# Turning normalised rows in 32x32 blocks on VectorE and in the loads, instead of on TensorE, for two of four token groups

## The chip, the cores and the metric

One core of a Trainium2 chip runs the whole program. The metric is the device time of one launch in microseconds; the median of three runs before the change was 2038.86 us (2037.51 to 2039.26).

## The reference, cut to what matters

One decoder layer over 2048 prompt positions and 64 sample positions, width 1024, in fp32. The part that matters here is the hand-over from the mixer to the MLP:

```python
x = layer_norm(DEEPNORM_ALPHA * x + g1 * mix, ln1_g, ln1_b)
h2 = x * (1.0 + sc2) + sh2
f = jnp.einsum("btf,fd->btd", jnp.square(jax.nn.relu(jnp.einsum("btd,df->btf", h2, w_up))), w_down)
x = layer_norm(DEEPNORM_ALPHA * x + g2 * f, ln2_g, ln2_b)
```

The mixer's output rows have tokens on partitions, since the norm runs along the features. The up projection needs h2 with features on partitions. Something has to turn the rows.

## The kernel before, in words

**Two phases.** The 2048 prompt positions are four groups (`SUPERS` = 4) of 512 (`GT`), four tiles of 128 rows each; the 64 sample rows are a fifth tile of the last group. First all four groups go through the mixer (`mixer(s)`, L1367 on PE and L1900 on VectorE), then all four through the MLP. Between the phases the normalised rows rest in DRAM, in `x_norm`, one row per position.

**Weights.** Every weight passes as a slab of 512 KB (128 partitions x 4 KB), in one fixed order numbered g. SP loads slab g into one of three raw buffers (L645), once POOL is done with slab g - 3. ACT copies it to the high part (`hi_part`, L1007), once PE is done with slab g - 4, of four slots. POOL subtracts to get the low part, in two halves (`lo_part`, L903). PE multiplies high by high, high by low and low by high (`mm3`, L1241 to L1243). A mixer has 24 slabs: 0 to 3 for v, 4 to 15 feature slabs (F0 to F11), 16 to 23 the output projection. A product slab of the MLP ("K", 12 matmuls of 512 columns) is one of seven products of a Strassen step on the down projection; an up slab ("U") has 24 matmuls. A group's MLP has 8 blocks of 4 U and 7 K. `mlp_order` (L65) fixes the order: U0 U1 K0 K1 U2 K2 K3 K4 U3 K5 K6 inside a group, with the K of the block before; at the end of a group seven K slabs stand in a row and then four U.

**The end of a mixer.** VectorE forms the residual and the statistics of each tile (L1893, L1895, L1658). ACT normalises tiles 0 and 1 in `xt` (`o_normal`, L1079), VectorE tiles 2 and 3 (L1668). The affine of this norm is folded into `scale2` and `bias2` for the MLP's input and applied on its own for the residual. In the next mixer SP stores the four tiles to `x_norm` behind slab 9 (`store_n`, L704) and reloads `xt` with the next residual behind slab 13. SP's queue also carries, into the third mixer, jobs that prepare sums of the down weights (L660, L674). VectorE writes the mixer's results to `mix` (`mix_out`, L1780) from feature slab F2 on; when it waits, its later evacuations of PSUM wait with it, and PE waits for those in turn by a ring of four banks.

**The start of an MLP group.** Group 0 is turned on PE while the last mixer ends. For groups 1 to 3, `next_n` (L801) loads the four row tiles of the coming group into four tiles that are free then (`next_rows`, L414: `gs`, `xt` tile 4, and two thirds of `rows`): tiles 0 and 1 behind U3 of the sixth block, 2 and 3 behind U3 of the eighth. After the last two K slabs of the seventh block and the first six of the eighth (`feature_after`, L121), PE turns one feature tile of 128 x 512 with four transposes of 128 x 128 into PSUM bank 2 or 3 (`n_transposes`, L1553; L1561), ACT applies `scale2` and `bias2` in place (`n_features`, L1137; L1141) and copies the high part to `hA` (L1145), VectorE subtracts for the low part (`n_feature`, L1707; L1711). The up projection of the next group waits for each of the eight parts (L1479).

**Order.** Nothing is scheduled by a planner: each engine's order is written out by hand, and SP is one queue in which an instruction that waits holds up every later transfer, the weight slabs among them.

Of the kernel before, what the change touches and what calls it, by code (L numbers as in the profile page):

```python
# [5 lines left out]
F32 = mybir.dt.float32  # L6
# [144 lines left out]
O_PAIRS = [(2, 3), (0, 1), (6, 7), (4, 5)]  # L151
MIX_ORDER = [0, 2, 3, 6, 1, 7, 4, 5]
# [148 lines left out]
def decoder_layer_kernel(nc, x_prompt, x_sample, x_turned, xs_turned, c_turned, conv_turned, pool_turned,  # L301
# [3 lines left out]
                         mod_rows, x_norm, w_mix):  # L305
    ctx = ExitStack()
    with ctx:
# [55 lines left out]

        ada_early = nc.alloc_sbuf_tensor_at("ada_early", [P, 2, KD, ADA_COLS], F32, offset=mix0)
# [124 lines left out]
        n_stage = sem("n_stage")  # L489
        n_in = [sem(f"n_in{t}") for t in range(5)]  # L490
# [90 lines left out]
        def _(sp):  # L581
# [123 lines left out]

            def store_y(s, t):
# [66 lines left out]
            for s in range(1, SUPERS):  # L773
                for n in range(MIX_SLABS):
                    slab(MIX_SLABS * s + n)
                    if n == 9:
                        store_n(s - 1)
                    if n == 13:
                        sp.wait_ge(n_stored, 64 * s)
                        load_residual(s)  # L780
# [20 lines left out]
            def next_n(s, t):  # L801
# [3 lines left out]
                elif s:  # L805
                    sp.wait_ge(n_tr, KD * s)
# [4 lines left out]
                sp.dma_start(next_rows[t], n_rows(s + 1, t)).then_inc(n_stage, 16)  # L811

            def load_n(s, t):
# [3 lines left out]
                if t == 4:  # L817
                    sp.wait_ge(n_tr, KD * (SUPERS - 1))
# [6 lines left out]
            for n, (kind, b, i) in enumerate(MLP_ORDER):  # L825
# [16 lines left out]
                else:  # L842
                    if (r, i) == (1, 1):

                        sp.wait_ge(n_tr, KD * s)
# [149 lines left out]
        def _(act):  # L995
# [141 lines left out]
            def n_features(e, k):  # L1137

                act.wait_ge(n_tr, KD * (e - SUPERS - 1) + k + 1)
                x = ps[:, 2 + k % 2, :]  # L1140
                act.activation(x, x, ACT.Identity, bias=bias2[:, k, 0:1], scale=scale2[:, k, 0:1]  # L1141
# [20 lines left out]
            for s in range(SUPERS):  # L1162
                nt, g0 = tiles_of(s), MIX_SLABS * s
                for n in range(MIX_SLABS):
                    if n == 3:
                        if s:
                            o_normal(s - 1, 0)
                            o_normal(s - 1, 1)
# [70 lines left out]
        def _(pe):  # L1239
# [313 lines left out]
            def n_transposes(s, k):  # L1553

                pe.wait_ge(n_stage, 64 * (s + 1))
                if k >= 2:
                    pe.wait_ge(x_split, KD * (SUPERS + s + 1) + k - 1)
                elif s == 0:
                    pe.wait_ge(h2s_split, 1)
# [22 lines left out]
            for kind, b, i in MLP_ORDER:  # L1582
# [9 lines left out]
                if k is not None:  # L1592
                    n_transposes(b // BLOCKS, k)
# [3 lines left out]
        def _(dve):  # L1597
# [181 lines left out]

            def mix_out(s, nt, k, x):  # L1780
                n = width(nt)
                signal(split(mix[:, 0, k, 0:n], mix[:, 1, k, 0:n], x), mix_ready, 8 * s + MIX_ORDER.index(k) + 1)

# [116 lines left out]
            def mixer(s):  # L1900
                nt, first = tiles_of(s), s == 0
                for pos, t in enumerate(v_order(nt)):
# [51 lines left out]
                for t in range(2, nt):  # L1954
                    x = xt[0:rows_of(t), t, :]
                    signal(normalise(x, x, t, ln_end), xn_dve, 2 * s + t - 1)

# [307 lines left out]
```

## Time and profile before

| what | value |
|---|---|
| median of 3 runs | 2038.86 us (2037.51 to 2039.26) |
| the profiled execution, its own time | 2037.39 us |
| its span, first to last instruction | 2035.6 us |
| PE, weight loads, VectorE busy | 99%, 83%, 70% |
| ACT, POOL busy | 44%, 72% |
| data moved | 357.5 MB, mean 176 GB/s |

PE is TensorE's matmuls, PEld its weight loads beside them, DVE is VectorE, ACT ScalarE, POOL GpSimd, and SPq the queue of SyncE, which issues nearly all transfers. Times are from the start of the span. PE ends the last mixer at about 634 us; the MLP groups change at about 966, 1297 and 1628 us. A row of the timeline has start, duration, engine, source line, what is written and read, and in brackets the idle time before it and what ended it.

### The profile page before, as it was taken

Reading aid. Unit: us, or ns where it says so; the run is one execution under the profiler, and the core shown is the slowest. Engines: PE = TensorE matmul, PEld = TensorE weight load, DVE = VectorE, ACT = ScalarE, POOL = GpSimd, SP = SyncE. Lnnn points to the kernel's source line nnn. Section 1 sums busy time; section 2 is a strip of 40 time slices with the busy share of each in tenths; the row PEclk is TensorE's granted clock in tenths of the full one; section 3 lists DMA queues with packets and bytes.
Section 4 is the critical chain, followed back from the end, with each engine's and each line's share of the span. In section 5 each row is a group of like instructions: output and inputs, shape, how many; then the busy total and the mean of one; then the engine's idle time right before and its main releaser. Section 6 shows DMA issues by size and latency. Waiting matters only on the chain.

```text
span 2035.6 us, 27636 instructions
## 1 busy us (share of the span) xinstructions
PE 2010.5 (99%) x10310; PEld 1689.6 (83%) x10310; DVE 1429.2 (70%) x1866; ACT 896.0 (44%) x1242; POOL 1456.7 (72%) x1117
## 2 busy tenths in 40 slices
PE   8999999999999999999999999999999999999996
PEld 6778888888988888888888888888888899999995
DVE  2566696785856365677888576888667778775786
ACT  3322232222133654546555544664454655444442
POOL 4446898863434677778888787888787876666686
PEclk9999999999999999999999999999999999999998
DMA  9877887943424445545345545444554534454341
GB/s 350 284 254 249 276 277 227 297 147 128 150 94 129 165 140 174 177 137 183 126 146 188 199 161 175 145 138 162 199 195 137 182 108 138 140 187 145 125 145 47
DMA packets 134623, 357.48 MB, mean 176 GB/s; under 512 B 12785, under 2 KB 46490, under 8 KB 131418
## 3 DMA queue, kind: packets, MB, share of 16 engines
q1 hardware_dynamic: 133625, 352.58, 52.5%
q10 hardware_dynamic: 864, 3.15, 0.5%
q8 instruction: 82, 1.34, 0.3%
q14 instruction: 52, 0.42, 0.1%
HBM read 321.22 MB, written 34.44 MB: 175 GB/s over the span
## 4 chain that ended last, share of the span: by engine, by line
PE 93%; DVE 4%; DMA 1%; ACT 1%; POOL 0%; issue 0%; SPq 0%; DVEq 0%; ACTq 0%; POOLq 0%
PE ps L1241 30%; PE ps L1243 30%; PE ps L1242 30%; DMA w_raw<-in_w_in 1%; PE ps L1490 1%; PE ps L1252 1%; PE ps L1349 1%; PE ps L1561 1%; PE ps L1269 0%; DVE acc L1842 0%; DVE hid_a L1970 0%; DVE hid_b L1970 0%; DVE pair_sums L1992 0%; DVE pair_sums L1993 0%; DVE pair_sums L1989 0%
## 5 line engine op out<-in xcount | busy, mean ns | idle before, releaser
L903 POOL TENSOR_TENSOR w_hilo<-w_raw,w_hilo 128x512 fp32r<-128x512 f32 x890 | 1279.8, 1468 | 544.9 <-ACT w_hilo L1007 544.4
L1007 ACT ACTIVATE w_hilo<-w_raw 128x1024 fp32r<-128x1024 f32 x445 | 470.3, 1058 | 521.7 <-PE ps L1243 411.5
L1241 PE MATMUL ps<-hA,w_hilo 128*128 128x512 f32 (+1 forms) x1760 | 619.9, 352 | 0.8 <-DVE acc L1876 0.8
L1242 PE MATMUL ps<-hA,w_hilo 128*128 128x512 f32 (+1 forms) x1760 | 618.3, 351 | 0.0
L1243 PE MATMUL ps<-hA,w_hilo 128*128 128x512 f32 (+1 forms) x1760 | 618.2, 351 | 0.0
L1241 PEld LDWEIGHTS ps<-hA,w_hilo 128*128 128x128 f32 x1760 | 330.3, 188 | 45.7 <-issue 2.8
L1242 PEld LDWEIGHTS ps<-hA,w_hilo 128*128 128x128 f32 x1760 | 330.3, 188 | 41.4
L1243 PEld LDWEIGHTS ps<-hA,w_hilo 128*128 128x128 f32 x1760 | 330.3, 188 | 41.3
L2078 DVE TENSOR_TENSOR acc<-acc,ps 128x512 f32<-128x512 f32 x270 | 177.7, 685 | 69.3 <-PE ps L1243 66.1
L1241 PE MATMUL ps<-w_hilo,hid_a 128*128 128x512 f32 x450 | 177.9, 395 | 0.3 <-ACT more_sums L1203 0.3
L1097 ACT ACTIVATE htmp<-ps 128x512 f32<-128x512 f32 x96 | 57.4, 598 | 272.4 <-PE ps L1243 265.2
L1243 PE MATMUL ps<-w_hilo,hid_a 128*128 128x512 f32 x450 | 175.4, 390 | 0.0
L1242 PE MATMUL ps<-w_hilo,hid_a 128*128 128x512 f32 x450 | 175.4, 390 | 0.0
L1241 PE MATMUL ps<-w_hilo,hid_b 128*128 128x512 f32 x450 | 175.3, 390 | 0.0
L1243 PE MATMUL ps<-w_hilo,hid_b 128*128 128x512 f32 x450 | 175.3, 389 | 0.0
L1242 PE MATMUL ps<-w_hilo,hid_b 128*128 128x512 f32 x450 | 175.2, 389 | 0.0
L1988 DVE TENSOR_TENSOR pair_sums<-htmp 128x256 f32<-128x256 f32 x62 | 36.6, 591 | 184.2 <-ACT htmp L1107 183.9
L1241 PE MATMUL ps<-w_hilo,mix 128*128 128x512 f32 (+1 forms) x272 | 106.3, 391 | 0.0
L1242 PE MATMUL ps<-w_hilo,mix 128*128 128x512 f32 (+1 forms) x272 | 105.9, 389 | 0.0
L1243 PE MATMUL ps<-w_hilo,mix 128*128 128x512 f32 (+1 forms) x272 | 105.9, 389 | 0.0
L1241 PEld LDWEIGHTS ps<-w_hilo,hid_a 128*128 128x128 f32 x450 | 84.5, 188 | 18.2 <-issue 1.9
L1243 PEld LDWEIGHTS ps<-w_hilo,hid_a 128*128 128x128 f32 x450 | 84.5, 188 | 17.9
(234 smaller groups left out, 2774.1 us busy)
## 6 DMA issues: line engine op xcount, KB each, us to landing
w_raw<-in_w_up SPq DMA_DIRECT2D x128, 512.0 KB, 3.5
w_raw<-w_mix SPq DMA_DIRECT2D x124, 512.0 KB, 3.2
w_raw<-in_w_down SPq DMA_DIRECT2D x97, 512.0 KB, 3.6
w_raw<-in_w_in SPq DMA_DIRECT2D x64, 512.0 KB, 4.4
xt<-in_w_ada SPq DMA_DIRECT2D x20, 1024.0 KB, 7.5
w_raw<-in_w_out SPq DMA_DIRECT2D x32, 512.0 KB, 4.5
xt<-x_norm SPq DMA_DIRECT2D x19, 512.0 KB, 5.2
xt<-in_w_down SPq DMA_DIRECT2D x36, 256.0 KB, 5.1
```

The costliest lines, as they stand in the source:

```text
L903: ins = pool.tensor_tensor(W[:, g % SLOTS, 1, cols], raw[:, g % RAW, cols], W[:, g % SLOTS, 0, cols], ALU.subtract)
L1007: act.activation(W[:, g % SLOTS, 0, :], raw[:, g % RAW, :], ACT.Copy).then_inc(hi_done, 1)
L1097: act.activation(x[:, 0:GT], ps[:, f % 2, :], ACT.Relu).then_inc(up_read, 1)
L1241: pe.matmul(out, w_hi, x_hi, start=start, stop=False)
L1242: pe.matmul(out, w_hi, x_lo, start=False, stop=False)
L1243: return pe.matmul(out, w_lo, x_hi, start=False, stop=stop)
L1252: ins = pe.matmul(ps[q:q + 32, 1 + 2 * (u % 2), 0:ADA_COLS], siluT[:, k, :], buf[:, k, :], start=(k < 4), stop=(k >= 4))
L1349: ins = pe.matmul(out[q:q + 64, r * pair:r * pair + r], v[:, P * pair + q:P * pair + q + 64], w[0:r, 2 * pair + odd, :], start=True, stop= ...
L1490: pe.matmul(ps[:, 2 + h, :], x, W[:, w, part, HALF * p:HALF * p + HALF], start=start and part == 0, stop=False)
L1561: ins = pe.transpose(ps[:, 2 + k % 2, P * t:P * t + P], next_rows[t][:, P * k:P * k + P], ident[:, :])
L1988: do(dve.tensor_tensor(s1, a21, a22, ALU.add))
L2078: dve.tensor_tensor(a, a, src, ALU.add).then_inc(d_evac, 1)
```

## The change

For groups 1 and 2 (`s < TURNED`, the next group's number less one) the turning is divided in two. In the mixers VectorE transposes each normalised tile of 128 x 1024 within blocks of 32 x 32, in two instructions of 128 x 512, into a new tile `n_turned` that shares its place with the first part of `mix`: tiles 2 and 3 right after they are normalised, tiles 0 and 1 at the start of the next mixer, once ACT has normalised them, for which ACT's two instructions stand one slab earlier in mixers 2 and 3. SP stores the four tiles to a second buffer in DRAM, `n_blocks`, behind slab 10 of the next mixer, and VectorE waits for those stores before its first write to `mix` there. In the MLP, `next_n` fetches for groups 1 and 2 from `n_blocks`: each of the four loads becomes eight, of 32 partitions x 16 pieces x 32 floats, which put the blocks in their places, so that the four tiles of `next_rows` hold features on partitions, two feature tiles each. PE's transposes go for these two groups, and ACT's affine reads the loaded tile and writes PSUM. Group 3 is turned as before. Waits that counted PE's transposes (`n_tr`) count ACT's affine instead (`n_affine`) for the reuse of the tiles.

```diff
+BLK = 32
+TURNED = 2
+        n_turned = nc.alloc_sbuf_tensor_at("n_turned", [P, 4, D], F32, offset=mix0)
...
+            def store_turned(s):
+                sp.wait_ge(turned_ready, 4 * s)
+                for t in range(4):
+                    row = (s - 1) * GT + P * t
+                    sp.dma_start(n_blocks[row:row + P, :], n_turned[:, t, :]).then_inc(turned_stored, 16)
...
                     if n == 9:
                         store_n(s - 1)
+                    if n == 10 and s > 1:
+                        store_turned(s - 1)
...
                 elif s:
-                    sp.wait_ge(n_tr, KD * s)
+                    sp.wait_ge(n_affine, KD * s)
...
-                sp.dma_start(next_rows[t], n_rows(s + 1, t)).then_inc(n_stage, 16)
+                if s == TURNED:
+                    sp.dma_start(next_rows[t], n_rows(s + 1, t)).then_inc(n_stage, 16)
+                    return
+                sp.wait_ge(turned_stored, 64 * (s + 1))
+                blocks = n_blocks[s * GT:(s + 1) * GT, :].rearrange("(a p) f -> p a f", p=BLK)
+                for half in range(2):
+                    for c in range(P // BLK):
+                        f = 2 * P * t + P * half + BLK * c
+                        sp.dma_start(next_rows[t][BLK * c:BLK * c + BLK, GT * half:GT * half + GT].rearrange(
+                                         "p (a i) -> p a i", i=BLK),
+                                     blocks[:, :, f:f + BLK]).then_inc(n_part[t], 16)
...
             def n_features(e, k):
-                act.wait_ge(n_tr, KD * (e - SUPERS - 1) + k + 1)
-                x = ps[:, 2 + k % 2, :]
-                act.activation(x, x, ACT.Identity, bias=bias2[:, k, 0:1], scale=scale2[:, k, 0:1]
+                s, x = e - SUPERS - 1, ps[:, 2 + k % 2, :]
+                if s < TURNED:
+                    act.wait_ge(n_part[k // 2], 128 * (s + 1))
+                    if s == 0 and k < 2:
+                        act.wait_ge(h2s_split, 1)
+                    else:
+                        act.wait_ge(x_split, KD * (SUPERS + s + 1) + k - 1)
+                    src = next_rows[k // 2][:, GT * (k % 2):GT * (k % 2) + GT]
+                else:
+                    act.wait_ge(n_tr, k + 1)
+                    src = x
+                act.activation(x, src, ACT.Identity, bias=bias2[:, k, 0:1], scale=scale2[:, k, 0:1]
                                ).then_inc(n_affine, 1)
...
                 for n in range(MIX_SLABS):
+                    if s and n == (2 if s > 1 else 3):
+                        o_normal(s - 1, 0)
+                        o_normal(s - 1, 1)
                     if n == 3:
-                        if s:
-                            o_normal(s - 1, 0)
-                            o_normal(s - 1, 1)
...
                 k = feature_after(kind, b, i)
-                if k is not None:
-                    n_transposes(b // BLOCKS, k)
+                if k is not None and b // BLOCKS == TURNED:
+                    n_transposes(TURNED, k)
...
+            def turn_tile(s, t):
+                step(dve.transpose(n_turned[:, t, 0:HALF], xt[:, t, 0:HALF]))
+                dve.transpose(n_turned[:, t, HALF:], xt[:, t, HALF:]).then_inc(turned_ready, 1)
+
             def mix_out(s, nt, k, x):
                 n = width(nt)
+                if s > 1 and k == MIX_ORDER[0]:
+                    dve.wait_ge(turned_stored, 64 * (s - 1))
...
                 nt, first = tiles_of(s), s == 0
+                if s > 1:
+                    for t in range(2):
+                        dve.wait_ge(xn_act, 2 * s - 1 + t)
+                        turn_tile(s - 1, t)
...
                     signal(normalise(x, x, t, ln_end), xn_dve, 2 * s + t - 1)
+                    if s in (1, 2):
+                        turn_tile(s, t)
```

## Rows read from the trace of the kernel before

**Rows 1.** The page: busy time, and the chain that ended last by engine.

```profile
PE 2010.5 (99%) x10310; PEld 1689.6 (83%) x10310; DVE 1429.2 (70%) x1866; ACT 896.0 (44%) x1242; POOL 1456.7 (72%) x1117
...
PE 93%; DVE 4%; DMA 1%; ACT 1%; POOL 0%; issue 0%; SPq 0%; DVEq 0%; ACTq 0%; POOLq 0%
```

**Rows 2.** One stretch: us; busy (xcount) PE, PEld, DVE, ACT, POOL; clock; DMA; GB/s.

```profile
700.00:1625.00 925.00, 924.65 (x4122) 764.67 (x4121) 676.36 (x735) 492.41 (x633) 751.46 (x514) 1.00 0.50 165
```

**Rows 3.** Timeline of PE, 938 to 967 us: start, us, instruction, count.

```profile
938.00 0.39 PE L1241 MATMUL ps<-w_hilo,hid_a 128*128 128x512 f32 x1
...
940.72 0.27 PE L1561 MATMUL ps<-ident,gs 128*128 128x128 f32 x1
...
943.93 0.27 PE L1561 MATMUL ps<-ident,gs 128*128 128x128 f32 x1
...
966.34 0.39 PE L1241 MATMUL ps<-hA,w_hilo 128*128 128x512 f32 x1
```

**Rows 4.** Source line L1561, the transposes: min/median/max ns, first, last start.

```profile
L1561 PE MATMUL ps<-ident,rows x48: 272/272/273, 940.9 to 1625.1; 128*128 128x128 f32 x48
```

**Rows 5.** VectorE's groups by form: count, busy us, mean ns of one.

```profile
L1679 DVE TENSOR_TENSOR mix<-acc,mix 128x512 fp32r<-128x512 f32 x24 | 30.4, 1265 | 0.8
L1678 DVE CAST mix<-acc 128x512 fp32r<-128x512 f32 x24 | 18.6, 774 | 0.8
```

**Rows 6.** Timeline of VectorE, ends of the second and third mixer, idle in brackets.

```profile
346.70 0.70 DVE L1658 BATCH_NORM_STATS2 st<-ps 128x6 f32<-128x512 f32 x1 [5.65 <-PE ps L1243]
...
487.02 0.69 DVE L1658 BATCH_NORM_STATS2 st<-ps 64x6 f32<-64x512 f32 x1 [12.06 <-PE ps L1243]
```

**Rows 7.** Timeline: SP's queue and VectorE's first write to mix.

```profile
357.61 3.47 SPq L704 DMA_DIRECT2D x_norm<-xt  x4
...
362.49 1.91 SPq L674 DMA_DIRECT2D gs<-in_w_down  x2
...
376.57 1.04 DVE L1678 CAST mix<-acc 128x512 fp32r<-128x512 f32 x1
```

**Rows 8.** Timeline of SP's queue around the two loads of the first group.

```profile
837.77 0.43 SPq L811 DMA_DIRECT2D gs<-x_norm  x1
...
919.37 0.91 SPq L811 DMA_DIRECT2D rows<-x_norm  x2
```

**Rows 9.** DMA issues: KB each, median us from issue to landing.

```profile
w_raw<-w_mix SPq DMA_DIRECT2D x124, 512.0 KB, 3.2
x_norm<-xt SPq DMA_DIRECT2D x16, 512.0 KB, 5.8
```

**Rows 10.** Timelines of ACT, POOL and PE, the slab behind the first loads.

```profile
848.50 1.06 ACT L1007 ACTIVATE w_hilo<-w_raw 128x1024 fp32r<-128x1024 f32 x1 [1.66 <-PE ps L1243]
...
848.33 2.54 POOL L903 TENSOR_TENSOR w_hilo<-w_raw,w_hilo 128x512 fp32r<-128x512 f32 x2
...
856.40 0.39 PE L1241 MATMUL ps<-w_hilo,hid_a 128*128 128x512 f32 x1
```

**Rows 11.** Timeline of POOL, 940 to 961 us: 14 halves of seven slabs.

```profile
940.69 20.18 POOL L903 TENSOR_TENSOR w_hilo<-w_raw,w_hilo 128x512 fp32r<-128x512 f32 x14 [3.24 <-ACT w_hilo L1007]
```

**Rows 12.** SP's queue: gathering loads (source line), behind a store (timeline).

```profile
L674 SPq DMA_DIRECT2D gs<-in_w_down x28: 544/612/1573, 170.6 to 400.4; - x28
...
96.38 0.38 SPq L660 DMA_DIRECT2D w_mix<-xt  x1
...
97.36 0.98 SPq L594 DMA_DIRECT2D gs<-in_b_ada  x1
```

**Rows 13.** DMA view of four stretches: packets, MB, share of 16 engines.

```profile
q1 hardware_dynamic: 323, 0.04, 15.0%
...
q1 hardware_dynamic: 401, 0.05, 94.0%
...
q1 hardware_dynamic: 143, 0.04, 41.0%
...
q1 hardware_dynamic: 254, 0.26, 105.4%
```

More of the change, by code:

```diff
@@ L304, in decoder_layer_kernel @@
                          y_prompt, y_sample, o_conv_p, o_pool_p, o_conv_s, o_pool_s, o_v_s,
-                         mod_rows, x_norm, w_mix):
+                         mod_rows, x_norm, n_blocks, w_mix):
     ctx = ExitStack()
@@ L489, in decoder_layer_kernel @@
         n_stage = sem("n_stage")
+        n_part = [sem(f"n_part{j}") for j in range(4)]
+        turned_ready = sem("turned_ready")
+        turned_stored = sem("turned_stored")
         n_in = [sem(f"n_in{t}") for t in range(5)]
@@ L817, in load_n @@
                 if t == 4:
-                    sp.wait_ge(n_tr, KD * (SUPERS - 1))
+                    sp.wait_ge(n_tr, KD)
                 sp.dma_start(xt[0:rows_of(t), t, :], n_rows(s, t)).then_inc(n_in[t], 16)
@@ L843, in _ @@
                     if (r, i) == (1, 1):
-                        sp.wait_ge(n_tr, KD * s)
+                        sp.wait_ge(n_affine, KD * s)
                         load_ln(ln2_g, ln2_b)
@@ L1553, in n_transposes @@
             def n_transposes(s, k):
-                pe.wait_ge(n_stage, 64 * (s + 1))
+                pe.wait_ge(n_stage, 64)
                 if k >= 2:
                     pe.wait_ge(x_split, KD * (SUPERS + s + 1) + k - 1)
-                elif s == 0:
-                    pe.wait_ge(h2s_split, 1)
                 for t in range(4):
@@ L2260 @@
     args.append(nc.dram_tensor("x_norm", (SEQ + ST, D), F32).ap())
+    args.append(nc.dram_tensor("n_blocks", (TURNED * GT, D), F32).ap())
     args.append(nc.dram_tensor("w_mix", (4, BLOCKS, P, D), F32).ap())
```

## The prediction, made before the changed kernel was run

> **What bounds the kernel now.** The profile's page first [rows 1]: PE is busy 2010.5 of 2035.6 us, and the chain that ended last is 93% PE. One stretch sharpens this [rows 2]: from 700 to 1625 us, where the change takes its work away, PE is without work for 0.35 us in 925, at a granted clock of 1.00, the upper level. So an instruction taken off PE there is worth its whole pitch, if the next weight slab is ready earlier too. POOL, which makes each slab's low part, is busy 751 us of the same 925; it is the engine that comes next.
>
> The sum below is made against the profiled execution, 2037.4 us (span 2035.6 and 1.8 around it). The median of the runs shown is 2038.9, 1.5 us higher, and I add that at the end.
>
> **1. PE loses 64 transposes.** A product slab of the down projection takes from 938.00 to 940.72, 2.72 us [rows 3]. With four transposes ahead of it the pitch is 943.93 - 940.72 = 3.21. The eight sets of a group fill 940.72 to 966.34: 25.62 us for eight slabs that alone need 8 x 2.72 = 21.76, so 3.86 us per group. The trace has 96 such transposes (the 48 of the row, from the two tiles in rows, are half of them), 32 for each of three groups, up to 1625 us [rows 4]; two groups go: 2 x 3.86 = **7.7 us**. Nothing hides it, since PE does not wait there.
>
> **2. ACT and VectorE in the MLP.** ACT still does one affine and one copy per feature tile, only its source moves from PSUM to SBUF, and VectorE's subtract is unchanged. Cost nothing: ACT is busy 492 of 925 us there [rows 2].
>
> **3. VectorE turns 8 tiles, 16 instructions of 128x512.** The trace of before has no such instruction. The nearest are fp32 copies and subtracts from SBUF of the same size: 774 ns mean, 1265 the dearer [rows 5]. Say 0.8 us each, between 0.4 and 1.3, so 6.4 us for the eight of a group. They stand where VectorE waits for PE: 12.06 us before the statistics at 487.02, when the fourth mixer has begun, and 5.65 us before those at 346.70 in the third [rows 6]. Tiles 0 and 1 are scaled by ACT, whose two instructions are moved one slab (about 5 us) forward for it. The overrun of about 1 us in the third mixer meets statistics that PE needs only four slabs later. Cost 0; if the cover were gone, 16 x 0.8 = 13 us.
>
> **4. Eight stores of 512 KB, and a wait before the first write to mix.** In the third mixer the stores go behind slab 10 and two loads that end at 364.40 [rows 7], then come four stores at the 3.47 us that four took before, and 5.8 us until the last has landed [rows 9]: 373.7. VectorE's first write to mix starts at 376.57, so there is no wait, with 3 us to spare. The fourth mixer has no such loads in SP's queue and five tiles' work ahead of that write, so more room. Behind VectorE's wait stand its later evacuations, so each microsecond beyond would first eat the four banks' slack. The stores hold slab 11 back by 4 us; it is needed some five slabs later. Cost 0.
>
> **5. The loads, which decide the case.** For each of two groups, four loads of 512 KB become 32 of 64 KB, each 512 packets of 128 bytes: 16 behind U slab 3 of the sixth block, 16 behind that of the eighth. SP issues them in its one queue, ahead of the next weight slab, where two loads stood, the second pair in 0.91 us [rows 8]. Call T the time from the first of the 16 until the last is issued and read.
>
> How much T is hidden? First batch: SP starts it at 837.77. The slab behind it then lands 3.2 us after its issue [rows 9], ACT's copy takes 1.06 and POOL's two halves 2.54, so its low part is ready at 844.6 + T. PE starts that slab at 856.40; before, it was ready at 850.87 [rows 8, 10]. So **T up to 11.8 us costs nothing.** Second batch: start 919.37, ready at 926.2 + T, PE at 938.00: again 11.8. But nine product slabs follow each other there. PE without transposes takes 2.72 each and POOL 20.18/7 = 2.88 [rows 11], so eight slabs on, POOL is ready at 949.2 + T and PE arrives at 938.00 + 21.76 = 959.8: **T up to 10.5 us.** Each microsecond of T beyond is a microsecond of PE waiting, twice each: stall = 2(T - 11.8) + 2(T - 10.5), no term below 0.
>
> What is T? No load here has this shape, so three rows bound it. SP's own issue: 0.91 us for a pair of plain loads and 0.04 to the next, or a median of 0.61 and 0.04 for loads that gather pieces of 1 KB [rows 8, 12]: 16 are 7.6 or 10.5 us. The packets' own time: in a stretch of mostly small packets (38.0 to 39.8 us) 323 of them took 15.0% of 16 engines in 1.8 us, 13.4 ns each, so 8192 over 16 engines are 6.9 us; in a busy one (37.4 to 37.9) 401 took 94.0% of 0.5 us, 18.8 ns, 9.6 us [rows 13]. The supply of packets: after a transfer of 512 packets the second instruction behind it ended 1.58 us after it (98.34 against 96.76), which times 16 is 25.3 us, and from an empty queue (1.8 to 2.3) 143 packets passed in 0.5 us, which is 28.6 us for 8192 [rows 12, 13]. The first of these is a store of 1 KB pieces at full data rate, the second includes the start of the queue; both overstate it. So T lies between 7.6 and 28.6. I take **10.5**, by the gathering load, whose shape is nearest; issue and packets overlap. Stall 0.
>
> Against this speaks a rule. The trace has 13.4 to 18.8 ns for mostly small packets and no sign of a penalty, but those came from compact tables and from SBUF (L616, L619), while here pieces of 128 bytes lie 4 KB and more apart in HBM [rows 13]. The Trainium skill ("DMA: Bandwidth & Descriptors", Specifications) asks for at least 512 bytes per transfer and says that below it the engine does a read-modify-write. An estimate from that page of the Trainium skill, at its 27 GiB/s per engine, is 18 ns for 512 bytes and twice that with a read ahead of the write, which makes T some 18 us and the sum about +21 us instead of -7.7; what it would do by rows is the upper part of rival (b).
>
> **Sum:** 2037.4 - 7.7 = 2029.7 as profiled, 2031.2 as a median.
>
> **Rivals.**
> (a) *The batch is just longer than its cover, or POOL takes the gain.* T between 12.05 and 14.1 leaves a result within 0.2% (4.1 us), about what a measurement of this kernel can tell from no change. For: the second cover is only 10.5 us, and POOL's 2.88 per slab is slower than PE's 2.72. Against: the gathering load's pace. At T = 13.1 stall and gain cancel: 2038.9.
> (b) *Slower: the weight slab behind each batch comes late.* Place: PE's first product slab after U slab 3 of blocks 6 and 8 in the first two groups, four waits. Price 4T - 44.6 less 7.7. It decides from T = 13.1 and shows beyond 14.1. At 16 us (1 us per load) the stall is 19.4 and the time 2050.6; if a scattered packet takes twice the 18.8 ns of the busy small ones, T is 19.3 to 20: at 20 us 35.4 and 2066.6 (the rule of the Trainium skill above points here); at 25.3 56.6 and 2087.8. For: the packet-supply rows above, and scattered reads that no row shows. Against: the packets' own times, and 1 KB pieces of 4 KB rows that pass at full rate, 254 in 0.75 us (97.5 to 98.25) at a share of 105% [rows 13].
> (c) *VectorE is late in the mixers*: the wait on the stores in the third, or turning dearer than 1.3 us. For: 3 us of margin. Against: bank slack. At 3 us in each of two mixers it would give 2037.
>
> That the transposes stay is excluded by the diff, for two groups of three.
>
> **How the numbers follow.** Forecast (T below 12.05) 0.46; (a) 0.15; (b) with T from 14.1 to 20 0.22, above 20 0.11; (c) 0.06, half of it slower. That is 0.46 faster, 0.18 same, 0.36 slower. Faster cases hold 2028.5 to 2034.7; the low end allows for a gain 2 to 3 us over the transposes' own. The high end, 2066.6, is T = 20 and leaves out the last 0.11. The likeliest case's own range is 2028.5 to 2034.7.
>
> **What the profile after should show.** Right: 32 transposes left and none before 1600 us; PE's idle between 700 and 1300 us below 1 us; product slabs at 2.72 us through the eighth block; SP's 16 loads in 7 to 11 us; VectorE's 16 new instructions under 1.3 us each in former gaps. Wrong: ACT's copies waiting for the slab's DMA behind L645 right after each batch, PE starting its first product slab there late, loads at 1 us or more each, or packets of 128 bytes at 30 ns and over. A PE gap in the third or fourth mixer before the first output products would speak for (c).

## The result, and the profile after

The changed kernel took 2042.08 us (median of 15 runs, 2040.17 to 2045.07) against 2038.27 for the kernel before on the same chip. The ratio is 1.002, with a 95% interval of 1.0013 to 1.0027: slower by 3.8 us where 7.7 us of gain were forecast. One of the 15 runs of the kernel before took 10179.1 us; it does not move the median. The profiled execution took 2041.59 us, 4.2 more than that of before.

The page of the changed kernel, busy times and the chain that ended last, answers to [rows 1]:

```profile
PE 2006.1 (98%) x10246; PEld 1682.3 (82%) x10246; DVE 1454.1 (71%) x1882; ACT 896.0 (44%) x1242; POOL 1458.6 (72%) x1117
...
PE 72%; DVE 7%; ACT 1%; issue 1%; POOL 0%; DVEq 0%; ACTq 0%; POOLq 0%
...
L1274 PE MATMUL ps<-w_hilo,hid_a 128*128 128x512 f32 x450 | 177.4, 394 | 7.4 <-DVE acc L2122 6.9
L2032 DVE TENSOR_TENSOR pair_sums<-htmp 128x256 f32<-128x256 f32 x62 | 40.9, 660 | 178.3 <-ACT htmp L1131 178.0
```

The 64 transposes are gone (10310 less 10246 instructions), and PE is less busy. But the chain is now 72% PE, where it was 93%, and PE's product matmuls idle 7.4 us, of which 6.9 end with VectorE's instruction at L2122: the evacuation that adds a product bank of PSUM to the accumulators. Neither a load nor POOL is named.

The queue did what step 5 said. SP's timeline around the second batch of the first group:

```profile
921.17 0.34 SPq L651 DMA_DIRECT2D w_raw<-in_w_up  x1
921.61 8.72 SPq L833 DMA_DIRECT2D rows<-n_blocks  x16
930.38 0.97 SPq L651 DMA_DIRECT2D w_raw<-w_mix  x2
```

Sixteen loads are issued in 8.72 us (and 4.52 + 4.15 for the first batch), and the slab behind them is issued at 930.38 us. In the kernel before it was issued 7.9 us sooner, behind the pair of plain loads of [rows 8]:

```profile
922.48 0.32 SPq L645 DMA_DIRECT2D w_raw<-w_mix  x1
```

Now ACT, POOL, VectorE and PE in the changed kernel. ACT's timeline:

```profile
935.25 1.06 ACT L1031 ACTIVATE w_hilo<-w_raw 128x1024 fp32r<-128x1024 f32 x1 [5.71 <-DMA w_raw<-w_mix]
936.53 1.06 ACT L1031 ACTIVATE w_hilo<-w_raw 128x1024 fp32r<-128x1024 f32 x1 [0.22 <-DMA w_raw<-w_mix]
937.78 1.06 ACT L1031 ACTIVATE w_hilo<-w_raw 128x1024 fp32r<-128x1024 f32 x1 [0.19 <-DMA w_raw<-in_w_down]
```

POOL's:

```profile
936.38 13.25 POOL L927 TENSOR_TENSOR w_hilo<-w_raw,w_hilo 128x512 fp32r<-128x512 f32 x10 [4.23 <-ACT w_hilo L1031]
```

VectorE's:

```profile
941.75 1.22 DVE L2032 TENSOR_TENSOR pair_sums<-htmp 128x256 f32<-128x256 f32 x1 [6.12 <-ACT htmp L1131]
943.01 1.40 DVE L2033 TENSOR_TENSOR pair_sums<-htmp 128x256 f32<-128x256 f32 x1
944.33 1.51 DVE L2036 TENSOR_TENSOR pair_sums<-pair_sums,htmp 128x256 f32<-128x256 f32 x1
945.87 1.37 DVE L2037 TENSOR_TENSOR pair_sums<-htmp,pair_sums 128x256 f32<-128x256 f32 x1
947.28 1.29 DVE L2122 TENSOR_TENSOR acc<-acc,ps 128x512 f32<-128x512 f32 x2
```

And PE's:

```profile
945.40 0.39 PE L1276 MATMUL ps<-w_hilo,hid_b 128*128 128x512 f32 x1
948.11 0.47 PE L1274 MATMUL ps<-w_hilo,hid_a 128*128 128x512 f32 x1 [2.32 <-DVE acc L2122]
```

The `pair_sums` are sums and differences of activation tiles that the next product slabs read; `acc<-acc,ps` is the evacuation. In the kernel before, the same rows of VectorE, and in a second fence what POOL did ahead of them, were:

```profile
939.55 0.42 DVE L1988 TENSOR_TENSOR pair_sums<-htmp 128x256 f32<-128x256 f32 x1 [6.11 <-ACT htmp L1107]
940.01 0.42 DVE L1989 TENSOR_TENSOR pair_sums<-htmp 128x256 f32<-128x256 f32 x1
940.35 0.42 DVE L1992 TENSOR_TENSOR pair_sums<-pair_sums,htmp 128x256 f32<-128x256 f32 x1
940.80 1.46 DVE L1993 TENSOR_TENSOR pair_sums<-htmp,pair_sums 128x256 f32<-128x256 f32 x1
942.29 1.28 DVE L2078 TENSOR_TENSOR acc<-acc,ps 128x512 f32<-128x512 f32 x2
```

```profile
927.42 10.03 POOL L903 TENSOR_TENSOR w_hilo<-w_raw,w_hilo 128x512 fp32r<-128x512 f32 x8 [2.02 <-ACT w_hilo L1007]
```

POOL was done at 937.45 and paused for 3.24 us until 940.69 [rows 11]; in that pause VectorE's first three sums took 0.42 us each, and the fourth, beside POOL again, 1.46. Afterwards the same work of POOL starts late, runs without a pause from 936.38 to 949.63, and all four sums take 1.2 to 1.5 us: 5.5 us for the four in place of 2.7. VectorE combines two SBUF tensors there, and so does POOL. The whole trace of before says the same: of its 248 instructions that write `pair_sums`, 101 ran while POOL was idle throughout and took 0.42 to 0.43 us each, and 94 ran wholly inside POOL's work and took 1.40 us in the median (0.46 to 1.54). The Trainium skill ("SBUF — State Buffer", Who interferes with whom) says that a VectorE instruction with two inputs in SBUF contends with a GpSimd instruction that reads SBUF. The trace agrees: 0.42 us alone, 1.22 to 1.51 beside POOL, and 0.64 per evacuation, with one input in PSUM, in both cases.

So the weight slab came in time for PE, and what came late was an evacuation of VectorE, an instruction that no part of the change touches.

### The profile page after: what moved, and what is told of

It reads as the page before. It is cut to its first block, busy times and chain, and to the rows that moved or that the text cites. A ratio compares the mean times of both kernels' runs of the same rounds, so it can differ in the third digit from the quotient of the medians.

```text
span 2039.8 us, 27598 instructions
## 1 busy us (share of the span) xinstructions
PE 2006.1 (98%) x10246; PEld 1682.3 (82%) x10246; DVE 1454.1 (71%) x1882; ACT 896.0 (44%) x1242; POOL 1458.6 (72%) x1117
## 4 chain that ended last, share of the span: by engine, by line
PE 72%; DVE 7%; ACT 1%; issue 1%; POOL 0%; DVEq 0%; ACTq 0%; POOLq 0%
PE ps L1274 23%; PE ps L1276 23%; PE ps L1275 23%; PE ps L1523 1%; DVE hid_b L2014 0%; DVE htmp L1885 0%; DVE acc L1880 0%; DVE pair_sums L2036 0%; DVE mix L1710 0%; DVE pair_sums L2037 0%; DVE pair_sums L2033 0%; DVE acc L1879 0%; DVE hA L1742 0%; DVE pair_sums L2032 0%; DVE hid_a L2014 0%
## 5 line engine op out<-in xcount | busy, mean ns | idle before, releaser
L2122 DVE TENSOR_TENSOR acc<-acc,ps 128x512 f32<-128x512 f32 x270 | 177.6, 685 | 67.4 <-PE ps L1276 64.1
L2032 DVE TENSOR_TENSOR pair_sums<-htmp 128x256 f32<-128x256 f32 x62 | 40.9, 660 | 178.3 <-ACT htmp L1131 178.0
```

The lines of the kernel that those rows point to most:

```text
L2032: do(dve.tensor_tensor(s1, a21, a22, ALU.add))
L2122: dve.tensor_tensor(a, a, src, ALU.add).then_inc(d_evac, 1)
```

## The experiments

For the profile of each run two numbers are set beside the times: where the fourth mixer starts again after a short wait that every kernel has (549.78 us in the kernel before), and the time from there to the end of the span, which leaves most of the mixers out. Each ratio is to runs of the kernel before on the same chip, whose medians lay between 2037.6 and 2038.5 us. The last three columns come from one execution each, and such an execution lies up to 1.2 us from the median of its runs; e6, whose mixers are those of before, has 551.00 in the column "at 550" against 549.78. A difference of about 1 us in these columns is not resolved by itself.

The expectations use short names. Theory A: the batch of loads delays a slab, POOL's work moves beside VectorE's sums, both get slower and PE waits for an evacuation. Rival B: the packets of 128 bytes cost time wherever they stand. Rival C: without the transposes POOL's 2.88 us per slab sets the pace. Theory D: VectorE is nearly full in the run of product slabs, and its order there keeps the gain away. Rival E: moving VectorE's work out of the run makes the next group's start late.

| run | median, us | ratio to before (95%) | at 550 | rest | rest to before |
|---|---|---|---|---|---|
| before | 2038.3 | | 549.78 | 1485.8 | |
| after | 2042.08 | 1.0020 (1.0013, 1.0027) | 551.64 | 1488.2 | +2.3 |
| e1_spread_loads | 2043.96 | 1.0028 (1.0017, 1.0040) | 551.68 | 1490.5 | +4.7 |
| e2_early_stores | 2041.62 | 1.0018 (1.0009, 1.0027) | 550.57 | 1488.4 | +2.6 |
| e3_plain_loads | 2037.75 | 1.0001 (0.9993, 1.0010) | 550.97 | 1483.9 | -1.9 |
| e4_plain_held | 2043.24 | 1.0028 (1.0017, 1.0040) | 551.32 | 1489.0 | +3.2 |
| e5_plain_sums_later | 2037.38 | 0.9996 (0.9987, 1.0005) | 551.16 | 1484.2 | -1.6 |
| e6_before_sums_later | 2041.41 | 1.0015 (1.0006, 1.0023) | 551.00 | 1489.1 | +3.3 |
| e7_spread_in_run | 2037.85 | 1.0000 (0.9991, 1.0009) | 551.66 | 1484.4 | -1.4 |
| e8_spread_sums_later | 2037.17 | 0.9996 (0.9987, 1.0004) | 551.64 | 1484.3 | -1.6 |
| e9_sums_two_late | 2037.93 | 0.9997 (0.9988, 1.0006) | 551.75 | 1483.7 | -2.2 |
| e10_sums_shifted | 2038.01 | 0.9999 (0.9990, 1.0008) | 551.31 | 1484.1 | -1.7 |
| e11_mixers_only | 2040.01 | 1.0007 (0.9998, 1.0016) | 552.66 | 1485.9 | +0.1 |
| e12_stores_by_act | 2037.66 | 0.9998 (0.9989, 1.0007) | 552.36 | 1484.2 | -1.6 |

### Is it the late slab, or the small packets?

e3_plain_loads and e4_plain_held go together. In e3 each tile comes by one plain load of `x_norm`, so this kernel leaves out the turning of the rows for groups 1 and 2:

```diff
-                for half in range(2):
-                    for c in range(P // BLK):
-                        f = 2 * P * t + P * half + BLK * c
-                        sp.dma_start(next_rows[t][BLK * c:BLK * c + BLK, GT * half:GT * half + GT].rearrange(
-                                         "p (a i) -> p a i", i=BLK),
-                                     blocks[:, :, f:f + BLK]).then_inc(n_part[t], 16)
+                sp.dma_start(next_rows[t], n_rows(s + 1, t)).then_inc(n_part[t], 16)
```

> The changed kernel with each tile fetched by one plain load of 512 KB of rows, as before the change, so that the MLP input of groups 1 and 2 is taken from rows that are not turned (that part of the computation is changed); transposes still gone, mixers as changed. Gives what the change is worth in the MLP if its loads cost nothing. Theory A: about 2032.7 us, PE idle near nothing at the group changes, product slabs at 2.72 us. Rival B (packets of 128 bytes as such): the same here, so this run says nothing against it alone. Rival C (POOL sets the pace without transposes): 2036 to 2040, with PE idle behind POOL in the run of product slabs.

e4 adds a wait to that:

```diff
                         next_n(s, r - 4)
+                        if s < TURNED and r == 7:
+                            sp.wait_ge(slab_used, SLAB["K", b - 1, 3] + 1)
```

> The kernel with plain loads, and behind the second pair of loads of groups 1 and 2 SP waits until PE is done with the fourth product slab of the seventh block, so that the next weight slab is issued about as late as behind the batch of small loads (the same part of the computation is changed). No small packets at all. Theory A: the late slab alone brings the loss back, about 4.5 us per group: pair sums of VectorE at 1.2 to 1.5 us each, PE idle of 2.3 and 1.2 us before two product slabs, 2032.7 + 9 = about 2041.5 us. Rival B (the small packets do it): 2032.7, no slow pair sums.

e3 took 2037.75 us and e4 2043.24. The wait of SP's queue, without a single small packet, costs 5.5 us, more than the whole loss of the change. VectorE's timeline in e4 is that of the changed kernel:

```profile
941.09 1.55 DVE L2028 TENSOR_TENSOR pair_sums<-htmp 128x256 f32<-128x256 f32 x1 [6.11 <-ACT htmp L1127]
942.67 1.40 DVE L2029 TENSOR_TENSOR pair_sums<-htmp 128x256 f32<-128x256 f32 x1
944.00 1.51 DVE L2032 TENSOR_TENSOR pair_sums<-pair_sums,htmp 128x256 f32<-128x256 f32 x1
945.54 1.37 DVE L2033 TENSOR_TENSOR pair_sums<-htmp,pair_sums 128x256 f32<-128x256 f32 x1
```

POOL's in e4 too:

```profile
936.06 13.24 POOL L923 TENSOR_TENSOR w_hilo<-w_raw,w_hilo 128x512 fp32r<-128x512 f32 x10 [4.56 <-ACT w_hilo L1027]
```

PE waits 2.64 us before 947.78 there, and 1.83 before 1279.46 in the next group. In e3 the first three sums are fast, and the wait at that place is 1.04 us:

```profile
940.73 0.43 DVE L2026 TENSOR_TENSOR pair_sums<-htmp 128x256 f32<-128x256 f32 x1 [6.10 <-ACT htmp L1125]
941.19 0.42 DVE L2027 TENSOR_TENSOR pair_sums<-htmp 128x256 f32<-128x256 f32 x1
941.53 0.42 DVE L2030 TENSOR_TENSOR pair_sums<-pair_sums,htmp 128x256 f32<-128x256 f32 x1
```

Theory A stands in this half: the late slab is enough for the slow sums and the waits.

Not all of e4's 5.5 us is waiting. After its wait of 2.64 us PE's matmuls from 948.9 to 951.9 us followed each other at 0.43 us in place of 0.23, and the granted clock fell towards the lower of its two levels; a window of e4, whose clock stands after the busy times:

```profile
950.00:953.00 3.00, 3.00 (x10) 2.31 (x10) 2.93 (x5) 2.60 (x5) 2.54 (x2) 0.66 0.54 178
```

The same came after the wait at 1279 us (0.50 from 1280 to 1283), and once in e2_early_stores after a wait of 2.45 us (0.59 from 948 to 951). The profiled execution of the changed kernel waited 2.32 us there and kept 1.00. It also had a second wait of 1.23 us, which e4 and e2 did not have behind the slow stretch, so the price of the clock can't be told apart from the wait that it replaced. Other executions of the changed kernel probably had such stretches: its four slowest runs (2043.23 to 2045.07 us) had a mean granted clock of 0.994 or 0.995, the other eleven 0.996 or 0.997.

The other half of the expectation for e3, 2032.7 us, does not stand: even with loads that cost nothing the change gains nothing.

The small loads themselves are tried in place. e1_spread_loads puts two behind each of eight slabs for the first batch and three behind each of six for the second:

```diff
+            pieces = {}
+            for s in range(TURNED):
+                for t0, first, per in ((0, ("U", BLOCKS * s + 5, 3), 2), (2, ("K", BLOCKS * s + 6, 1), 3)):
+                    for j in range(16):
+                        pieces.setdefault(MLP_ORDER.index(first) + j // per, []).append((s, t0 + j // 8, j % 8))
...
                 slab(MLP0 + n)
+                for piece in pieces.get(n, []):
+                    next_n(*piece)
```

> The changed kernel with its 32 small loads per group spread out: two behind each of eight slabs from U slab 3 of the sixth block, three behind each of six slabs from the second product slab of the seventh block, all before the run of nine product slabs. Same loads, same packets, no slab held back by more than 1.5 us. Theory A (the batch of 16 shifts the slab chain, POOL then works without a pause while VectorE forms its pair sums, both get slower together, and PE waits for VectorE's evacuations): PE's idle of some 5.2 and 4.3 us at the two group changes goes, the four pair sums that took 1.2 to 1.5 us each at 942 to 947 us take about 0.42 each for the first three, and the time falls from 2042.1 to about 2032.7 us. Rival B (the packets of 128 bytes themselves slow the engines or the slabs, wherever they stand): no better than 2040. Rival C (without the transposes POOL's 2.88 us per slab sets the pace of the nine product slabs): 2036 to 2038, PE idle in the run of product slabs behind POOL.

It took 2043.96 us, the worst of all, and not by the mechanism of A, B or C: the second batch was begun too early. Its tiles are free only when the first norm's gains have been applied, and SP stood in that wait. SP's timeline:

```profile
900.56 0.33 SPq L651 DMA_DIRECT2D w_raw<-w_mix  x1
913.37 1.39 SPq L837 DMA_DIRECT2D rows<-n_blocks  x3
914.80 0.49 SPq L651 DMA_DIRECT2D w_raw<-in_w_up  x1
```

No slab was issued for 14 us, and PE waited 1.97 us for POOL at 923. From 560 up to 913 us, with the first batch spread, PE did not wait once. e7_spread_in_run starts the second batch four slabs later:

```diff
-                for t0, first, per in ((0, ("U", BLOCKS * s + 5, 3), 2), (2, ("K", BLOCKS * s + 6, 1), 3)):
+                for t0, first, per in ((0, ("U", BLOCKS * s + 5, 3), 2), (2, ("K", BLOCKS * s + 6, 4), 2)):
```

> The changed kernel with its small loads spread two behind a slab: the first 16 from U slab 3 of the sixth block (as in the spread kernel before, where PE did not wait there), the second 16 from the fifth product slab of the seventh block on, two behind each of eight slabs, after the point where the place is free (in the spread kernel before SP stood still for 12.3 us for it). Theory A and D together: nothing is late any more, and the time is that of the plain loads, 2037.5 to 2039. Rival B (the small packets cost something wherever they stand): 2040 to 2042.

2037.85 us, within 0.1 us of the plain loads and 0.6 of the kernel before. The 8192 packets of 128 bytes per batch cost nothing that these runs resolve when no slab stands behind more than two of their loads. Rival B is out. So the loss is a matter of where in one queue the loads stand. That the gain stays away needs another cause.

### Where is the gain?

e7 and e3 have no transposes for the two groups, no late slab, and no gain. Their waits are in the run of product slabs: in e7 1.04, 0.81 and 0.30 us in the first group, again all behind VectorE's evacuations. Counted as pitch beyond 0.2275 us per matmul, and without what the kernel before has too, e3 loses 5.6 us by its waits in the two groups, 4.9 of them behind VectorE's evacuations and the rest behind ACT, and 7.7 less 5.6 is 2.1, close to the 1.9 by which the rest of its span is shorter. One stretch of three kernels, 939 to 970 us, in the order PE, PEld, DVE, ACT, POOL; first before, then after, then e3:

```profile
939.00:970.00 31.00, 31.00 (x154) 25.59 (x153) 28.76 (x36) 22.50 (x29) 27.96 (x20) 1.00 0.52 167
```

```profile
939.00:970.00 31.00, 27.11 (x115) 20.98 (x115) 27.58 (x32) 22.31 (x29) 28.71 (x22) 1.00 0.58 173
```

```profile
939.00:970.00 31.00, 29.76 (x130) 23.76 (x129) 27.74 (x36) 23.35 (x30) 28.13 (x19) 1.00 0.50 153
```

VectorE was busy 28.76 of 31 us before the change, and POOL 27.96. PE was the bound there, but VectorE had only 2.24 us left in 31, less than the 3.86 us per group that PE's work shrank by; the transposes filled time in which PE would otherwise have waited for VectorE. Theory D was made from this, and tried by taking VectorE's sums over the accumulators out of the run:

```diff
-                    return {1: [0], 3: [1], 5: [2], 6: [3, 4]}.get(i, [])
+                    return {6: [0, 1, 2, 3, 4]}.get(i, [])
```

With plain loads this is e5:

> The kernel with plain loads (its MLP input for groups 1 and 2 comes from rows that are not turned), and VectorE's sums over the accumulators, which stand after the second, fourth, sixth and seventh product slab at each group's end, all moved behind the seventh. Theory D (VectorE, 28.8 of 31 us busy in the run of product slabs before the change, sets the pace once the transposes are gone; the plain loads alone gave 2037.75 with 2.2 and 3.3 us of PE waiting for evacuations): two of its instructions of 1.7 to 2.4 us and one of 2.1 leave the run, PE's waits behind VectorE there fall under 1 us per group, and the time falls by 3 to 5 us, to 2033 to 2035. Rival C (POOL, 28.1 of 31 us busy, is as full as VectorE and sets 2.88 us per slab anyway): a gain below 1 us, 2037 or more. Rival E (the moved sums make the next group's start late): 2038 to 2042.

With the kernel before it is e6:

> The kernel before with only that move of VectorE's sums behind the seventh product slab. Theory D: PE with its transposes takes 3.21 us per slab and never waited for VectorE, so nothing is gained: 2037.9, within 0.1%. Rival E (the moved sums make the next group's start late): 2040 to 2044.

And with the small loads spread as in e7 and the early stores of e2, the full result, it is e8:

> All of it together, computing the full result: the small loads spread as in the kernel with two per slab, the stores of the third mixer behind slab 8, and VectorE's sums behind the seventh product slab. Theories A and D: the gain of e5 with the loads hidden, 2032.5 to 2035, faster than both kernels. Rival B or E: 2038 to 2042.

e5 took 2037.38 us, e8 2037.17, e6 2041.41. In the run the theory holds: PE's waits there fall from three to one per group in e8 (1.04 us at 949, 1.04 at 1279), and the product slabs follow each other at 2.72 us, as ACT's copies, each of which PE releases, show in e8:

```profile
957.96 1.06 ACT L1043 ACTIVATE w_hilo<-w_raw 128x1024 fp32r<-128x1024 f32 x1 [0.36 <-PE ps L1288]
...
960.68 1.06 ACT L1043 ACTIVATE w_hilo<-w_raw 128x1024 fp32r<-128x1024 f32 x1 [0.35 <-PE ps L1288]
...
963.40 1.06 ACT L1043 ACTIVATE w_hilo<-w_raw 128x1024 fp32r<-128x1024 f32 x1 [0.36 <-PE ps L1288]
```

That is below 2.88, and none of PE's waits in the MLP of e3, e5, e7 or e8 ends with POOL, so rival C is out as well. But what was saved there is lost some 20 to 50 us later. VectorE's timeline of e8 behind the run has the sum that follows the five, which now all stand behind the seventh slab (it started at 974.34 us in the kernel before), and directly behind it the `pair_sums`:

```profile
978.16 2.20 DVE L2159 TENSOR_TENSOR acc<-acc,more_sums 128x1024 f32<-128x1024 f32 x1
980.39 1.40 DVE L2044 TENSOR_TENSOR pair_sums<-htmp 128x256 f32<-128x256 f32 x1
981.82 1.40 DVE L2045 TENSOR_TENSOR pair_sums<-htmp 128x256 f32<-128x256 f32 x1
983.14 1.50 DVE L2048 TENSOR_TENSOR pair_sums<-pair_sums,htmp 128x256 f32<-128x256 f32 x1
984.68 1.40 DVE L2049 TENSOR_TENSOR pair_sums<-htmp,pair_sums 128x256 f32<-128x256 f32 x1
```

Three of these four are slow in the kernel before too (0.65, 1.40, 1.51 and 1.40 us), but there VectorE had 3.28 us to spare ahead of them:

```profile
978.85 0.65 DVE L1988 TENSOR_TENSOR pair_sums<-htmp 128x256 f32<-128x256 f32 x1 [3.28 <-ACT htmp L1107]
```

In e8 PE then waits 0.54 us at 988 and 0.27 and 0.38 at 1013 and 1017 for ACT, which takes VectorE's late results. Rival E is right as well, and e6 shows it alone: the moved sums cost the unchanged kernel 3 us, in waits of 1.21 and 0.40 us at 1015 and 1019 and the same one group on.

Two more orders were tried between the two, both with the low part of the first turned tile behind the next two evacuations. e9 puts one sum behind the fifth slab and four behind the seventh:

```diff
+                    return {4: [0], 6: [1, 2, 3, 4]}.get(i, [])
...
                     down(b, i)
+                if feature_after(kind, b, i) == 1:
+                    n_feature(s, 0)
...
-                if k is not None:
+                if k:
                     n_feature(s, k)
```

> The kernel with loads two per slab and early stores, full result, with two changes in VectorE's order at a group's end: the first sum over the accumulators goes behind the fifth product slab of the run and the other four behind the seventh (before: second, fourth, sixth, seventh, seventh), and the low part of the first turned feature tile goes behind the two evacuations after it, so that PE's wait of 1.04 us at 948 us for the accumulator shrinks by 0.69. Theory D (VectorE's order in the run of product slabs is what keeps the change from paying): the waits in the run fall to under 0.8 us per group; moving only part of the sums leaves less at the next group's start than the 1.9 us per group there when all stood behind the seventh: 2034 to 2036. Rival (the sums cost the same wherever they stand, since VectorE has no room on either side): 2037 or more.

e10 shifts each by two slabs at most:

```diff
+                    return {3: [0], 5: [1], 6: [2, 3, 4]}.get(i, [])
```

> The same, with the first sum behind the fourth product slab, the second behind the sixth and the other three behind the seventh. Theory D: less work lands behind the run than in the kernel with two late, more stands in it, where VectorE had gaps of 0.71 us per slab; 2034 to 2036.5. Rival (no room on either side): 2037 or more.

2037.93 and 2038.01 us, neither to be told from the kernel before. The wait of 1.04 us at 949 became two of 0.31 and 0.68. The rest of the span is 1483.7 us in e9, 2.2 less than before and the least of all, though e3, e5, e8 and e10 lie within 0.6 of it; 7.7 were hoped for. The rival, no room on either side, is nearer than theory D.

### What do the mixers cost?

In the changed kernel PE waits 1.21 us at 427 for VectorE's write to `mix`. Two timelines of VectorE in the third mixer, before and after, show how it falls behind:

```profile
398.55 0.71 DVE L1842 TENSOR_TENSOR acc<-acc 128x524 f32<-128x524 f32 x1
399.29 0.70 DVE L1844 TENSOR_TENSOR acc<-acc 128x520 f32<-128x520 f32 x1
400.03 0.69 DVE L1845 TENSOR_TENSOR acc<-acc 128x512 f32<-128x512 f32 x1
```

```profile
377.38 0.65 DVE L1709 CAST mix<-acc 128x512 fp32r<-128x512 f32 x1 [0.47 <-DMA n_blocks<-n_turned]
...
398.03 1.68 DVE L1880 TENSOR_TENSOR acc<-acc 128x524 f32<-128x524 f32 x1
399.75 1.67 DVE L1882 TENSOR_TENSOR acc<-acc 128x520 f32<-128x520 f32 x1
401.45 1.67 DVE L1883 TENSOR_TENSOR acc<-acc 128x512 f32<-128x512 f32 x1
```

It is the same thing again: 0.7 us each while POOL pauses (397.96 to 400.82 us), 1.67 beside its subtractions (396.15 to 402.57 us). Three runs look at the cause. e2 moves the stores:

```diff
-                    if n == 10 and s > 1:
+                    if s > 1 and n == (8 if s == 2 else 10):
                         store_turned(s - 1)
```

> The changed kernel with the four stores of turned tiles in the third mixer behind slab 8 in place of slab 10; all else the same. The mixers lose 1.87 us against the kernel before (start of a matmul at 550.59 against 548.72). Theory A (the wait of 0.47 us for the stores and the slab that they hold back put POOL's work beside VectorE's sums, which took 1.67 us in place of 0.7, and PE waits 1.2 us at 427): the loss falls below 0.6 us and the time from 2042.1 to about 2040.5. Rival (the turning itself, 11 us more on VectorE, makes it late): 2042.1 and the same 1.9 us late at 550.

e11 keeps the changed mixers and gives the MLP back its plain loads and all its transposes:

```diff
-                if s == TURNED:
-                    sp.dma_start(next_rows[t], n_rows(s + 1, t)).then_inc(n_stage, 16)
-                    return
+                sp.dma_start(next_rows[t], n_rows(s + 1, t)).then_inc(n_stage, 16)
+                return
...
-                if k is not None and b // BLOCKS == TURNED:
-                    n_transposes(TURNED, k)
+                if k is not None:
+                    n_transposes(b // BLOCKS, k)
```

> The mixers as changed (VectorE's 16 turning instructions, the eight stores behind slab 10, the wait before the first write to mix), and the MLP as before the change: plain loads, all transposes on PE. The second copy is stored and never read. It prices the mixers' part by itself. Theory: 0.6 to 1.9 us more than before, 2039 to 2040, by the wait for VectorE's write to mix at 427 us (0.5 to 1.2 us). Rival (the mixers cost nothing and all of the loss is in the MLP): 2038, within 0.3 us. Rival (the mixers cost the whole 3.8 us): 2042.

e12 is e8 with the stores issued by ACT:

```diff
+                    if n == 4 and s > 1:
+                        act.wait_ge(turned_ready, 4 * s - 4)
+                        for t in range(4):
+                            row = (s - 2) * GT + P * t
+                            act.dma_start(n_blocks[row:row + P, :], n_turned[:, t, :]).then_inc(turned_stored, 16)
```

> The kernel with loads two per slab and VectorE's sums behind the seventh product slab, full result (2037.17 us with its stores in SP's queue), but the eight stores of turned tiles are issued by ACT, where it idles for 7 us before it normalises v (352 to 359 us in the third mixer), so that no weight slab waits for them in SP's queue. Theory (in the third mixer it is the late slabs, copied at 373.6 and 376.2 us in place of 369.1 and 372.5, that move POOL's work beside VectorE's sums, 1.67 us each in place of 0.71, and VectorE's backlog then stops PE for 1.2 to 1.5 us at 427): the three sums at 398 to 403 us take 0.7 to 0.95 us again, PE's wait at 427 us is below 0.5 us, and the time is 2035.5 to 2036.5, the mixers' 1.6 us given back. Rival (the turning and the traffic of the stores themselves delay the mixers, whichever queue issues them): 2037 or more, and the wait at 427 us stays above 1 us.

e11 took 1.6 us more than the kernel before in the median, with an interval from 0.9998 to 1.0016, so the mixers' price is between nothing and 3 us, likeliest 1.6. e2 gained 0.5 us, within its uncertainty; its wait at 426 fell to 0.48 us, but e8 and e9 have the same early stores and waits of 1.22 and 1.51. e12 gained nothing: two of the three sums did go back (1.68, 0.70 and 0.69 us) and the wait fell to 0.68 us, yet the slabs were as late (ACT's copies at 373.45 and 376.10 us, against 373.56 and 376.19 with SP's stores in e9). The four stores to `x_norm` behind slab 9 took SP longer, beside those that ACT had issued:

```profile
360.59 5.11 SPq L710 DMA_DIRECT2D x_norm<-xt  x4
```

That is 5.11 us against 3.47 in [rows 7]; the two loads ahead of them took 2.71 us in place of 1.54. A wait of 0.48 us at 426 also stands in e6, whose mixers are those of before, so one profile can't settle a difference of this size. How much of the mixers' 1.6 us is the wait for the stores, how much the late slabs and how much the turning stays open.

## Why the prediction was wrong, step by step

**Step 1, the transposes, failed as a statement of worth.** PE did lose them and a product slab does take 2.72 us without them, so the 7.7 us are right as work. "Nothing hides it, since PE does not wait there" was the error. It follows from [rows 2] that an instruction more on PE costs its pitch, not that one less gains it: that needs the slack of the next engine in that very stretch. The prediction named POOL as the engine that comes next and set no bound by VectorE; of VectorE it had only the average of [rows 2], 676 of 925 us busy, while in the eight slabs that shrink it was 28.76 of 31. With loads that cost nothing (e3) the rest of the span is 1.9 us shorter, and 2.2 in the best order found (e9), each from one execution. So of this term some 1.4 to 2.2 us came back in the orders tried, and in e3 5.6 of the 7.7 went into waits, 4.9 of them for VectorE.

**Step 2** was right for ACT (896.0 us busy in both kernels). For VectorE it named only the subtract, which is unchanged, and not what ran around it.

**Step 3** was right. The turning instructions took 0.67 to 0.71 us each, where 0.8 was taken; in the third mixer they end at 346.4 us, in the former gap.

**Step 4 was nearly right and yet not free.** VectorE waited 0.47 us where 3 us of room were forecast. The stores were issued by 367.74 us, as forecast (364.40 + 3.47). The term that was too small is the landing: 5.8 us is a median, and the last of these four took 10.7 us from its issue and landed at 377.29, where 373.7 was forecast. "The stores hold slab 11 back by 4 us; it is needed some five slabs later" counted when PE needs it and not what POOL does when it comes. The mixers together cost about 1.6 us by e11, not well resolved.

**Step 5 was right in its mechanism and its size, and wrong in what it left out.** T comes out of the low part's time: 938.94 = 926.2 + 2.2 (the later start) + T gives 10.5 us, the value taken; for the first batch 858.38 = 844.6 + 1.9 + T gives 11.9, of which 1 us is POOL's second half (2.27 us, where 1.28 is usual), and PE waited 0.2 us there. The packets of 128 bytes were not dear: their median was 13 ns, and in e7 they cost nothing that can be resolved. The rule on 512 bytes in the Trainium skill ("DMA: Bandwidth & Descriptors", Specifications), by which the prediction estimated T at 18 us, did not show in these reads into SBUF. But the cover of 10.5 us was measured to the moment when PE would starve for a slab. Well before that, the late slabs put POOL's work beside VectorE's sums, and PE starved for an evacuation: waits that, counted as pitch beyond 0.2275 us per matmul and without one at 1016 to 1019 us that both kernels have, come to 5.4 us in the first group and 4.4 in the second. 9.8 less 7.7 is 2.1, of the 2.3 us that the rest of the span grew; the other 1.9 of the profile's 4.2 passed before 550 us.

Together: the profile missed the forecast by 11.9 us (2041.59 against 2029.7). Waits that e3 has too, with loads that cost nothing, are 5.6 us of it, 4.9 for VectorE (step 1); the further waits behind the late slab are 4.2 (step 5); and 1.9 passed before 550 us (step 4 and scatter, not separated).

**The rivals.** (a) held the sum nearly right (POOL or a batch just too long takes the gain) and named the wrong engine; POOL's 2.88 us per slab was no bound, since slabs follow at 2.72 in e8. (b) looked behind the right batch, but the waits stand before the third and the fourth product slab, not the first, and its cause was wrong: T was never above 13.1. One of the signs of (b) did show, ACT's copy waiting 5.71 us for the slab's DMA, without PE starving for that slab. (c), VectorE late, was sought in the mixers alone. A rival that asks what POOL and VectorE do to each other when one is shifted was missing, and the trace of before held it: sums of one shape at 0.42 and 1.46 us side by side, the fast ones in POOL's pause.

## What to carry to other kernels

An engine at 100% says what one more instruction costs; what one less gains is bounded by the slack of the next engine in that stretch, read from a window as narrow as the work removed (here 2.24 us of VectorE's in 31, of which about 1 us per group came back). Where a queue delays a transfer, follow it past its first consumer: a delay that starves nobody can still move one engine's work beside another's and slow both. When one shape of instruction has two durations in a trace, find out what stands beside the slow one before its neighbours are moved.

## What the hardware showed that was not expected

VectorE's sums and differences of two SBUF tensors took 0.42 us (128x256) and 0.7 us (128x512) while POOL paused, and 1.4 and 1.67 us beside POOL's subtractions of 128x512: 2.4 to 3.3 times as long, whereas its additions with one PSUM input, 0.64 us each in pairs, and its 32x32 turning, 0.67 to 0.71 us with POOL busy or not, did not change. After a wait of 2.64 us, and after one of 1.83, PE's granted clock fell to the lower level (e4: 0.66 from 950 to 953 us, 0.50 from 1280 to 1283). Loads of 64 KB in 512 packets of 128 bytes, from rows 4 KB apart, took 0.49 us of issue each in the median and landed in 2.2 us. With four stores issued by ACT shortly before, four of SP's own took 5.11 us in place of 3.47, so a second queue gave them no room of their own here.
